# First attention of a decoder trunk: query weights loaded by whole depth, one unit for each group of heads, with the groups' scores placed between them

## The chip, the core and the metric

The kernel runs on one core of a Trainium2 chip. The core has a matrix engine (TensorE, PE in the profile, with its weight loads as PEld), VectorE (DVE), ScalarE (ACT), GpSimd (POOL) and an engine that issues most loads (SyncE, SP). The metric is the device time of one execution in microseconds; lower is better. Data lies in an on-chip memory of 128 partitions; TensorE writes its sums into eight banks, each of 128 partitions by 512 float32.

## The reference, cut to what matters

Two decoder layers and a final norm on x of shape (1, 256, 1024), all float32. Layer 0 is sliding-window attention with 16 heads of 64, 2 key and value heads, window 128, a learned sink logit per head and a relative bias, followed by a dense SwiGLU. Layer 1 is stick-breaking attention, followed by eight experts with top-2 routing. The change touches the first attention alone:

```
qkv = h @ w_qkv + b_qkv              # h = rms_norm(x): 256 x 1024, w_qkv: 1024 x 1280
q, k, v = split(qkv, [1024, 1152])   # 16 query heads, 2 key heads, 2 value heads of 64
s = einsum('bnqhgd,bnkhd->bnhgqk', q, kb) * 64 ** -0.5
s = where(valid, s + bias, -inf)     # kb: a block of 128 keys and the block before it
p = softmax(concat([s, sink]))[..., :-1]
o = einsum('bnhgqk,bnkhd->bnqhgd', p, vb)
x = x + o.reshape(...) @ w_o
```

## The kernel before, in words

**Weights come in units.** A unit is 1 MB of a weight matrix: 512 of its rows by 512 of its columns, or (what the code calls whole depth) all 1024 rows by 256 columns. SyncE loads a unit into one of seven `raw` buffers. ScalarE rounds it into `high` (`make_high`, L565), VectorE makes the remainder `low` = raw - high (`make_low`, L570), and TensorE multiplies with both: a product of float32 quality is three matmuls (high x high, high x low, low x high; L1542 stands for all matmuls that go through the helper). There are three `high` and three `low` buffers, so the rounding of unit n waits until TensorE has used unit n - 3, and the load of unit n waits until `low` of unit n - 7 is made. Units are numbered in the order of use: 0 and 1 hold the key and value columns (half as wide), 2 to 5 (`AT["q0"]` to `AT["q0"] + 3`) the query columns, 6 to 9 the output projection `wo0`, 10 and up the dense layer. `ENDS` says by which event a unit counts as used: a bank filled, or a count.

**Every engine has its own written order.** Each engine runs its program from top to bottom and waits on semaphores. `split_to(n)` in ScalarE's and VectorE's programs makes all units up to n that are not made yet, so where such a line stands decides what waits behind it. `plan()` assigns each result a bank and its turn in it; a writer waits until the bank's earlier contents are freed (`begin`), a reader until they are filled (`full`), and others until they are taken out (`taken`).

**The first attention.** The 16 heads are worked on in four groups g of four heads. For each group:

- TensorE fills `("q", g)` (256 query columns by 256 tokens).
- VectorE's `queries(g)` (L1191, L1196) scales it, adds the bias and writes `qT`.
- TensorE's `swa_scores(g)` fills four banks: `s1` (tokens 128 to 255 against 256 keys) and `s0` (tokens 0 to 127 against 128 keys).
- VectorE's `biased(g)` (L1208) adds bias and mask, which empties the banks; `shifts(g)` (L1218 to L1224) finds the rows' peaks.
- ScalarE takes the exponentials (L858).
- VectorE's `inverses(g)` (L1229 to L1231) and `probabilities` (L593) normalize; for group 1 GpSimd does the latter.
- TensorE's `swa_transpose(g)` (L1751) turns the probabilities into three banks, which ScalarE copies out (`probs_transposed`, L869).
- TensorE's `swa_values(g)` fills `("oT0", g)`, which ScalarE and VectorE split into the next product's input (`input_part_high` L827, `input_part_low` L1105).

The keys and values, each first turned upside down by a matmul (`keys_and_values_flipped`), come from VectorE's `kv_rows` (L1178); VectorE copies the keys into `kT_swa` (L1185) and the tokens' scale into `spread` (L1133).

Before the change, units 2 and 3 hold columns 0 to 511 of the queries (rows 0 to 511, then 512 to 1023), so groups 0 and 1 are both complete only near the end of unit 3, and the keys' flip stands between the two units. Then TensorE does `swa_scores(0)` and `swa_scores(1)`, units 4 and 5 (groups 2 and 3), `swa_scores(2)`, `swa_transpose(0)`, `swa_scores(3)`, `swa_transpose(1)`, `swa_values(0)`, `swa_values(1)` and unit 6, the first of `wo0`, which begins with the input that came from group 0 and needs group 1's from its third step of four. After unit 6 comes `swa_transpose(2)`, then unit 7, then `swa_transpose(3)` and the values of groups 2 and 3, then units 8 and 9.

**Loads around it.** SyncE's order is: x, units 0 and 1, the constants, units 2 and 3, then a wait for the bias rows (`rows_stored`: VectorE's table of 16 rows, written to memory by a GpSimd DMA), the load of `hankel` from them (16 x 128 pieces of 512 bytes on 128 partitions' side), units 4 and 5, `wo0`, and so on. GpSimd makes the bias mask from `hankel`.

Of the kernel before, what the change touches and what calls it, by code (L numbers as in the profile page):

```python
# [14 lines left out]
P = 128  # L15
# [57 lines left out]
def unit_ends():  # L73
# [4 lines left out]
    def add(name, *keys):  # L78
        at[name] = len(ends)
        ends.extend(keys)  # L80

    add("kv0", None, ("kv", 0))
    add("q0", None, ("q", 1), None, ("q", 3))
# [96 lines left out]
def plan():  # L180
# [6 lines left out]
    u.use("columns", 2)  # L187
    u.use(("R", 0), 1)
    u.use("k", 2)
    u.use(("q", 0), 4)  # L190
    u.use(("q", 1), 5)
    u.use("v", 6)

    def swa_scores(g, banks):
        for half in range(2):
            u.use(("s1", g, half), banks[half])
        for half in range(2):
            u.use(("s0", g, half), banks[2 + half])
# [4 lines left out]

    swa_scores(0, (0, 1, 2, 7))
    swa_scores(1, (3, 6, 4, 5))
    u.use(("q", 2), 0)
    u.use(("q", 3), 1)
    swa_scores(2, (2, 7, 3, 6))
    swa_transposes(0, (4, 5, 0))
    swa_scores(3, (2, 7, 3, 6))  # L210
    swa_transposes(1, (1, 4, 5))
    u.use(("oT0", 0), 0)
    u.use(("oT0", 1), 2)
    for tb, bank in enumerate((7, 3)):
        u.use(("wo0", 0, tb), bank)
    swa_transposes(2, (1, 5, 0))
    for tb, bank in enumerate((6, 4)):
        u.use(("wo0", 1, tb), bank)
    swa_transposes(3, (1, 5, 0))
    u.use(("oT0", 2), 2)  # L220
    u.use(("oT0", 3), 1)
# [98 lines left out]
def build(nc, a):  # L320

    ctx = ExitStack()
    with ctx:
# [280 lines left out]
        def _(sp):  # L604
# [39 lines left out]
            columns(AT["q0"], w, 0, HALF)  # L644
# [3 lines left out]
            columns(AT["q0"] + 2, w, HALF, 2 * HALF)  # L648
# [99 lines left out]
        def _(act):  # L748
# [95 lines left out]
            split_to(AT["kv0"] + 1 + SPLIT)  # L844
            b = full(act, "v")
            freed(nc.scalar.copy(v_swa[:, :, :].rearrange("p t s -> p (t s)"), b[:, 0:TB * KV * HD]), "v")
            split_to(AT["q0"] + SPLIT)
# [28 lines left out]
            probs_transposed(1)  # L876
            exponentials(2, range(GROUP // 2), True)
            input_part_high("oT0", 0)
            input_part_high("oT0", 1)
# [150 lines left out]
        def _(dve):  # L1030
# [205 lines left out]
            split_to(AT["kv0"] + 1 + SPLIT)  # L1236
            dve.wait_ge(minus_sinks_ready, 1)
            queries(0)
            queries(1)
            biased(0)  # L1240
            shifts(0)
            split_to(AT["q0"] + SPLIT)
# [3 lines left out]
            inverses(0)  # L1246
            queries(3)
            split_to(AT["q0"] + 1 + SPLIT)
            inverses(1)
            biased(2)  # L1250
            shifts(2)
# [288 lines left out]
        def _(pe):  # L1540
# [188 lines left out]
            by_features([("q", 0), ("q", 1)], AT["q0"], keys_and_values_flipped)  # L1729
# [37 lines left out]

            taken(pe, "k")
            swa_scores(0)
            swa_scores(1)  # L1770
            by_features([("q", 2), ("q", 3)], AT["q0"] + 2)
            swa_scores(2)
            swa_transpose(0)
            swa_scores(3)
            swa_transpose(1)
            taken(pe, "v")
            swa_values(0)
            swa_values(1)
# [300 lines left out]
```

## Time and profile before

| | |
|---|---|
| time, median of 3 runs | 1384.54 us (1384.53 to 1385.44) |
| profiled execution, its own time | 1387.25 us |
| span of that execution, first to last instruction | 1385.4 us |
| mean granted TensorE clock | 0.994 |
| TensorE busy | 1365.2 us (99%) |
| VectorE busy | 1126.9 us (81%) |
| ScalarE busy | 921.1 us (66%) |
| `low` L570, 397 instructions | 898.2 us, 2274 ns each |
| read from memory | 421.57 MB |

The page has six parts: busy time by engine; the span in 40 slices; the DMA queues; the chain of work that ended last, followed back from the end; the costliest groups of instructions, each with the idle time of its engine before it and what ended it; and the DMA issues. The first attention lies between about 17 and 94 us of the span. In the slices a digit is a busy share in tenths, for PEclk the granted share of TensorE's full clock of 2.4 GHz. A busy TensorE is not one at its best rate: at half the clock it counts as busy too.

### The profile page before, as it was taken

The page shows a single profiled execution, that of the slowest core. Times are in us where ns is not written, and L with a number is a line of the kernel's source. Part 1 is how long each engine was busy: PE and PEld are TensorE (multiplying, and loading weights), DVE is VectorE, ACT ScalarE, POOL GpSimd, SP SyncE. Part 2 cuts the span into 40 slices and gives each one's busy share as a digit, 9 for nine tenths or more (in the row PEclk, how much of TensorE's full clock was granted, in tenths as well). Part 3 has the DMA queues.
Part 4 walks back from the last instruction along what each step waited for, and adds up shares of the span by engine and source line. Part 5 has one row for each costly group of instructions (what it writes and reads, how often), then busy time and mean ns, then how long its engine had stood idle before and what let it go on. Part 6 is the DMA issues. An engine that isn't in the chain of part 4 may idle for free.

```text
span 1385.4 us, 18580 instructions
## 1 busy us (share of the span) xinstructions
PE 1365.2 (99%) x6770; PEld 1138.3 (82%) x6770; DVE 1126.9 (81%) x893; ACT 921.1 (66%) x766; POOL 41.9 (3%) x39
## 2 busy tenths in 40 slices
PE   8899999999999999999999999999999999999997
PEld 7788888898778888888888888888888888888885
DVE  5867666576458888888888888888898888889886
ACT  5664433544546777777777777777777777777775
POOL 2000000000000000000100000000000000000000
PEclk9999999999999999999999999999999999999999
DMA  9455654755148999999999999999999999999993
GB/s 309 164 173 192 205 176 148 232 183 186 44 149 327 386 377 349 394 385 360 371 393 387 347 394 371 375 372 390 374 363 395 375 354 383 395 373 366 391 371 123
DMA packets 197321, 429.52 MB, mean 310 GB/s; under 512 B 7046, under 2 KB 36976, under 8 KB 197280
## 3 DMA queue, kind: packets, MB, share of 16 engines
q1 hardware_dynamic: 193776, 417.63, 82.9%
q0 software_dynamic: 2944, 10.16, 2.6%
q10 hardware_dynamic: 560, 1.16, 0.3%
q8 instruction: 28, 0.46, 0.1%
q14 instruction: 13, 0.11, 0.0%
HBM read 421.57 MB, written 7.36 MB: 310 GB/s over the span
## 4 chain that ended last, share of the span: by engine, by line
PE 92%; DVE 5%; issue 1%; ACT 1%; DMA 1%; DVEq 0%; SPq 0%
PE bank L1542 89%; DVE low L570 2%; PE bank L1987 2%; DMA raw<-in_swa_w_qkv 1%; PE bank L1956 0%; DVE work L1463 0%; PE bank L1585 0%; PE bank L1751 0%; DVE work L1208 0%; DVE peak L1218 0%; DVE h L1070 0%; DVE h L1208 0%; DVE qT L1191 0%; DVE h L593 0%; PE bank L1916 0%
## 5 line engine op out<-in xcount | busy, mean ns | idle before, releaser
L570 DVE TENSOR_TENSOR low<-raw,high 128x2048 fp32r<-128x2048 f32 (+1 forms) x397 | 898.2, 2274 | 168.7 <-ACT high L565 166.6
L565 ACT CAST high<-raw 128x2048 fp32r<-128x2048 f32 (+1 forms) x397 | 754.7, 1902 | 287.2 <-PE bank L1542 276.3
L1542 PE MATMUL bank<-high,inT 128*128 128x512 f32 (+1 forms) x2032 | 647.1, 391 | 6.6 <-DVE low L570 2.6
L1542 PEld LDWEIGHTS bank<-high,inT 128*128 128x128 f32 x2032 | 381.7, 188 | 87.9 <-DVE low L570 5.4
L1542 PE MATMUL bank<-low,inT 128*128 128x512 f32 (+1 forms) x1016 | 394.7, 388 | 0.0
L1542 PEld LDWEIGHTS bank<-low,inT 128*128 128x128 f32 x1016 | 191.7, 189 | 37.5
L1542 PE MATMUL bank<-high,hid_high 128*128 128x512 f32 x528 | 207.2, 393 | 0.0
L1542 PE MATMUL bank<-high,hid_low 128*128 128x512 f32 x528 | 205.7, 390 | 0.0
L1542 PE MATMUL bank<-low,hid_high 128*128 128x512 f32 x528 | 205.5, 389 | 0.0
L1542 PE MATMUL bank<-inT,high 128*128 128x512 f32 (+1 forms) x704 | 190.7, 346 | 0.3 <-DVE inT L1114 0.3
L1542 PE MATMUL bank<-inT,low 128*128 128x256 f32 x544 | 144.4, 280 | 0.0
L1542 PEld LDWEIGHTS bank<-inT,high 128*128 128x128 f32 x704 | 119.1, 189 | 14.2 <-issue 0.7
L1542 PEld LDWEIGHTS bank<-high,hid_low 128*128 128x128 f32 x528 | 99.1, 188 | 21.0
L1542 PEld LDWEIGHTS bank<-low,hid_high 128*128 128x128 f32 x528 | 99.2, 188 | 20.2
L1542 PEld LDWEIGHTS bank<-high,hid_high 128*128 128x128 f32 x528 | 99.2, 188 | 19.9
L1542 PEld LDWEIGHTS bank<-inT,low 128*128 128x128 f32 x544 | 103.0, 189 | 4.1
L999 ACT ACTIVATE work<-bank 128x512 f32<-128x512 f32 x56 | 33.6, 599 | 45.9 <-PE bank L1542 45.9
L1442 DVE TENSOR_TENSOR hid_low<-bank,hid_high 128x512 fp32r<-128x512 f32 x56 | 38.3, 683 | 0.0
L1463 DVE TENSOR_TENSOR work<-work,bank 128x512 f32<-128x512 f32 x56 | 38.1, 681 | 0.0
L982 ACT CAST hid_high<-bank 128x512 fp32r<-128x512 f32 x56 | 32.6, 583 | 2.8 <-PE bank L1987 2.8
L1987 PEld LDWEIGHTS bank<-consts,work 128*128 128x128 f32 x224 | 27.8, 139 | 7.2
L1987 PE MATMUL bank<-consts,work 128*128 128x128 f32 x224 | 33.5, 271 | 0.0
(194 smaller groups left out, 536.8 us busy)
## 6 DMA issues: line engine op xcount, KB each, us to landing
raw<-in_moe_w_gate SPq DMA_DIRECT2D x112, 1024.0 KB, 7.2
raw<-in_moe_w_up SPq DMA_DIRECT2D x112, 1024.0 KB, 7.5
raw<-in_moe_w_down SPq DMA_DIRECT2D x112, 1024.0 KB, 7.3
raw<-in_sb_w_qkv SPq DMA_DIRECT2D x12, 1024.0 KB, 5.1
raw<-in_ffn_w_down SPq DMA_DIRECT2D x11, 1024.0 KB, 4.9
raw<-in_ffn_w_gate SPq DMA_DIRECT2D x10, 1024.0 KB, 5.4
raw<-in_ffn_w_up SPq DMA_DIRECT2D x10, 1024.0 KB, 5.3
raw<-in_swa_w_qkv SPq DMA_DIRECT2D x4, 1024.0 KB, 11.1
```

What stands on the lines that cost most here:

```text
L565: nc.scalar.copy(high[n % SPLIT][:, :, 0:c], raw[r][:, :, 0:c]).then_inc(high_done, 1)
L570: nc.vector.tensor_tensor(low[n % SPLIT][:, :, 0:c], raw[n % RAW][:, :, 0:c], high[n % SPLIT][:, :, 0:c].bitcast(F32), ALU.subtract).then_ ...
L982: nc.scalar.copy(hid_high[:, half_of(b)], p).then_inc(input_high_ready, 1)
L999: freed(nc.scalar.activation(e_silu[b % 2], p[0:CAP, :], ACT.Silu), ("g", b))
L1442: freed(V.tensor_tensor(hid_low[:, half_of(b)], bank[:, USES[("hidT", b)][0], :], hid_high[:, half_of(b)].bitcast(F32), ALU.subtract), ("h ...
L1463: freed(V.tensor_tensor(e_prod[b % 2], e_silu[b % 2], p[0:CAP, :], ALU.mult), ("u", b))
L1542: return nc.tensor.matmul(out, lhsT, rhs, start=start, stop=stop, **kw)
L1987: ins = nc.tensor.transpose(out[:, s * CAP:(s + 1) * CAP], e_prod[b % 2][:, s * P:(s + 1) * P], ident[0:CAP, 0:CAP])
```

## The change

It does the following.

- The four query units become whole-depth units, each of 256 columns, one for each group: `deep_columns` in place of `columns`. Each run of memory that a load reads is 1 KB in place of 2 KB; the bytes are the same. A unit counts as used when its group's bank is filled.
- TensorE has `queries_of(g, middle)`: the two column halves of group g, 24 matmuls each, with `middle` between them. The middle of group 0 is the flip of keys and values; that of groups 1, 2 and 3 is the scores of the group before.
- `swa_scores(3)` still follows `swa_transpose(0)`; `swa_values(0)` now stands ahead of `swa_transpose(1)`.
- Banks are dealt out anew. The scores of groups 2 and 3 both use 2, 7, 3, 0.
- VectorE: `queries(0)` now precedes the remainder of unit 4, `queries(1)` follows `shifts(0)`, `biased(2)`, `inverses(1)`, `shifts(2)` precede `queries(3)`, and the remainder of unit 6 follows `queries(3)`.
- ScalarE: the copy of the values precedes the rounding of unit 4, and the first half of group 2's exponentials and group 0's input part precede the copies of group 1's transposes.

```
@@ unit_ends
-    add("q0", None, ("q", 1), None, ("q", 3))
+    add("q0", *[("q", g) for g in range(H // GROUP)])
@@ plan
+    u.use(("q", 0), 4)
+    u.use("k", 2)
+    u.use("v", 6)
     u.use(("R", 0), 1)
-    u.use("k", 2)
-    u.use(("q", 0), 4)
-    u.use(("q", 1), 5)
-    u.use("v", 6)
...
+    u.use(("q", 1), 5)
     swa_scores(0, (0, 1, 2, 7))
-    swa_scores(1, (3, 6, 4, 5))
-    u.use(("q", 2), 0)
+    u.use(("q", 2), 3)
+    swa_scores(1, (4, 5, 6, 0))
     u.use(("q", 3), 1)
-    swa_scores(2, (2, 7, 3, 6))
-    swa_transposes(0, (4, 5, 0))
-    swa_scores(3, (2, 7, 3, 6))
+    swa_scores(2, (2, 7, 3, 0))
+    swa_transposes(0, (4, 5, 6))
+    swa_scores(3, (2, 7, 3, 0))
+    u.use(("oT0", 0), 6)
     swa_transposes(1, (1, 4, 5))
-    u.use(("oT0", 0), 0)
-    u.use(("oT0", 1), 2)
+    u.use(("oT0", 1), 1)
...
@@ SyncE
-            columns(AT["q0"], w, 0, HALF)
+            deep_columns(AT["q0"], w, 0)
             sp.wait_ge(rows_stored, 16)
...
-            columns(AT["q0"] + 2, w, HALF, 2 * HALF)
+            deep_columns(AT["q0"] + 2, w, HALF)
@@ ScalarE
-            split_to(AT["kv0"] + 1 + SPLIT)
             b = full(act, "v")
             freed(nc.scalar.copy(v_swa[:, :, :].rearrange("p t s -> p (t s)"), b[:, 0:TB * KV * HD]), "v")
+            split_to(AT["kv0"] + 1 + SPLIT)
             split_to(AT["q0"] + SPLIT)
...
             probs_transposed(0)
-            probs_transposed(1)
             exponentials(2, range(GROUP // 2), True)
             input_part_high("oT0", 0)
+            probs_transposed(1)
             input_part_high("oT0", 1)
@@ VectorE
-            split_to(AT["kv0"] + 1 + SPLIT)
             dve.wait_ge(minus_sinks_ready, 1)
             queries(0)
-            queries(1)
+            split_to(AT["q0"] + 2)
             biased(0)
             shifts(0)
-            split_to(AT["q0"] + SPLIT)
+            queries(1)
+            split_to(AT["q0"] + 3)
             biased(1)
             shifts(1)
             queries(2)
             inverses(0)
+            biased(2)
+            inverses(1)
+            shifts(2)
             queries(3)
             split_to(AT["q0"] + 1 + SPLIT)
-            inverses(1)
-            biased(2)
-            shifts(2)
             biased(3)
@@ TensorE
-            by_features([("q", 0), ("q", 1)], AT["q0"], keys_and_values_flipped)
+            def queries_of(g, middle):
+
+                w = unit(AT["q0"] + g)
+                wh, wl = by_tiles(w[0]), by_tiles(w[1])
+                b = begin(pe, ("q", g))
+                for s in range(2):
+                    cols = slice(s * P, (s + 1) * P)
+                    for t in range(DT):
+                        ins = product(b[:, s * SEQ:(s + 1) * SEQ], (wh[:, t, cols], wl[:, t, cols]), inputs(t, every),
+                                      s == 0 and t == 0, t == DT - 1, skip_group_check=True)
+                    if s == 0:
+                        middle()
+                filled(ins, ("q", g))
...
+            queries_of(0, keys_and_values_flipped)
             taken(pe, "k")
-            swa_scores(0)
-            swa_scores(1)
-            by_features([("q", 2), ("q", 3)], AT["q0"] + 2)
-            swa_scores(2)
+            queries_of(1, lambda: swa_scores(0))
+            queries_of(2, lambda: swa_scores(1))
+            queries_of(3, lambda: swa_scores(2))
             swa_transpose(0)
             swa_scores(3)
-            swa_transpose(1)
             taken(pe, "v")
             swa_values(0)
+            swa_transpose(1)
             swa_values(1)
             from_heads(0)
```

## Rows read from the trace of the kernel before

**Rows 1.** The page: engines' shares of the chain of work that ended last.

```profile
PE 92%; DVE 5%; issue 1%; ACT 1%; DMA 1%; DVEq 0%; SPq 0%
```

**Rows 2.** TensorE's waits to 130 us: line, releaser, total us, times, longest.

```profile
PE bank L1542 <- DVE work L1208: 2.8, 1, 2.8
```

**Rows 3.** Chain that ended last, 15 to 80 us: start, length, what.

```profile
17.42 15.90 PE bank L1542 x130
...
53.81 2.93 PE bank L1542 x16
...
57.38 1.56 ACT work L869 x3
...
59.05 1.73 ACT work L858 x8
60.78 0.48 ACT inT L827
...
62.13 5.71 PE bank L1542 x24
...
69.14 5.73 PE bank L1542 x24
...
79.13 0.93 PE bank L1542 x3
```

**Rows 4.** Windows: length, busy of PE, PEld, DVE, ACT, POOL; clock; DMA share, GB/s.

```profile
53.35:56.76 3.41, 2.95 (x17) 2.51 (x18) 3.21 (x8) 0.00 (x0) 2.38 (x3) 0.50 0.98 303
...
406.00:408.00 2.00, 2.00 (x7) 1.48 (x8) 0.72 (x5) 2.00 (x2) 0.00 (x0) 0.50 0.97 381
```

**Rows 5.** Timeline of VectorE: start, length, line, out<-in, count, idle before it.

```profile
26.72 1.73 DVE L1185 COPY kT_swa<-bank 64x256 f32<-64x256 f32 x4 [3.06 <-PE bank L1542]
...
34.60 1.95 DVE L1208 TENSOR_TENSOR h<-bank,kv_area 128x512 f32<-128x512 f32 x4
36.68 1.22 DVE L1218 TENSOR_REDUCE peak<-h 128x4 f32<-128x1024 f32 x1
...
38.81 2.28 DVE L570 TENSOR_TENSOR low<-raw,high 128x2048 fp32r<-128x2048 f32 x1
41.01 1.94 DVE L1208 TENSOR_TENSOR work<-bank,kv_area 128x512 f32<-128x512 f32 x4
...
45.22 0.68 DVE L1191 TENSOR_TENSOR qT<-bank,gain_row 128x512 f32<-128x512 f32 x1
...
46.47 0.16 DVE L1229 TENSOR_TENSOR total<-row_sum,sink_exp 128x8 f32<-128x8 f32 x1
...
48.65 0.68 DVE L1191 TENSOR_TENSOR qT<-bank,gain_row 128x512 f32<-128x512 f32 x1
```

**Rows 6.** Timeline of TensorE, 74 to 80 us.

```profile
74.71 1.47 PE L1751 MATMUL bank<-consts,h 128*128 128x128 f32 x12
76.11 1.52 PE L1542 MATMUL bank<-work,v_swa 128*64 128x256 f32 x12
77.46 1.47 PE L1542 MATMUL bank<-h,v_swa 128*64 128x256 f32 x12
```

**Rows 7.** DMA view, 12 to 15 us: packets of 2 KB.

```profile
DMA packets 585, 1.17 MB, mean 388 GB/s; under 512 B 16, under 2 KB 16, under 8 KB 585
```

**Rows 8.** DMA view, packets of 1 KB: 254 to 257, then 264 to 266.8 us.

```profile
DMA packets 1042, 1.07 MB, mean 356 GB/s; under 512 B 15, under 2 KB 1041, under 8 KB 1041
...
DMA packets 931, 0.94 MB, mean 336 GB/s; under 512 B 11, under 2 KB 931, under 8 KB 931
```

**Rows 9.** DMA view, 15 to 16 us: first packets of GpSimd's queue since 12.

```profile
q0 software_dynamic: 46, 0.04, 11.2%
```

**Rows 10.** Timeline of SyncE: the load of hankel, issued after the bias rows' store.

```profile
16.94 0.37 SPq L646 DMA_DIRECT2D work<-bias_dram  x1
```

**Rows 11.** Timeline of ScalarE: the rounding of unit 4.

```profile
26.82 1.91 ACT L565 CAST high<-raw 128x2048 fp32r<-128x2048 f32 x1 [5.48 <-DMA raw<-in_swa_w_qkv]
```

**Rows 12.** Timeline of GpSimd: the last piece of the bias mask.

```profile
26.67 1.08 POOL L714 TENSOR_SCALAR_AFFINE_SELECT kv_area<-work 128x1024 f32<-128x1024 f32 x1
```

More of the change, by code:

```diff
@@ L202, in swa_transposes @@
             u.use(("pT", g, t), bank)
+    u.use(("q", 1), 5)
     swa_scores(0, (0, 1, 2, 7))
-    swa_scores(1, (3, 6, 4, 5))
-    u.use(("q", 2), 0)
+    u.use(("q", 2), 3)
+    swa_scores(1, (4, 5, 6, 0))
     u.use(("q", 3), 1)
-    swa_scores(2, (2, 7, 3, 6))
-    swa_transposes(0, (4, 5, 0))
-    swa_scores(3, (2, 7, 3, 6))
+    swa_scores(2, (2, 7, 3, 0))
+    swa_transposes(0, (4, 5, 6))
+    swa_scores(3, (2, 7, 3, 0))
+    u.use(("oT0", 0), 6)
     swa_transposes(1, (1, 4, 5))
-    u.use(("oT0", 0), 0)
-    u.use(("oT0", 1), 2)
+    u.use(("oT0", 1), 1)
     for tb, bank in enumerate((7, 3)):
         u.use(("wo0", 0, tb), bank)
-    swa_transposes(2, (1, 5, 0))
-    for tb, bank in enumerate((6, 4)):
+    swa_transposes(2, (4, 5, 2))
+    for tb, bank in enumerate((6, 1)):
         u.use(("wo0", 1, tb), bank)
-    swa_transposes(3, (1, 5, 0))
+    swa_transposes(3, (0, 4, 5))
     u.use(("oT0", 2), 2)
-    u.use(("oT0", 3), 1)
+    u.use(("oT0", 3), 4)
     def transposed(name, banks):
```

## The prediction

> **What bounds the kernel now.** I read the page first. TensorE carries 92% of the chain that ended last [rows 1]. So a change here pays only if it takes away a wait of TensorE or a stretch at low clock, or lets a waiting chain of other engines end sooner; the number of matmuls stays the same. Second, the waits of TensorE up to 130 us: one stands out, 2.8 us, released by VectorE's `biased` (L1208) [rows 2]. The chain shows which: TensorE stops after `swa_transpose(0)` and starts `swa_scores(3)` at 53.81, when `biased(2)` has emptied the banks [rows 3]. Those scores then take 2.93 us [rows 3], because the granted clock is 0.50 of full (1.2 GHz) from 53.35 to 56.76, after TensorE had stood still since 51.0 [rows 4]. Behind them ScalarE copies the transposes (57.38), does half of group 2's exponentials (59.05, 1.73 us) and only then group 0's input (60.78), so `wo0` starts at 62.13 [rows 3]. Third, the timeline of VectorE: from 34.60, when `biased(0)` starts, its pieces follow one another without a pause, but before that it idled 3.06 us until 26.72, waiting for the keys' flip [rows 5]. So the stretch from 34 to 54 us is VectorE's; TensorE only looks full because its units fit beside it. From 62.13 on, the units of `wo0` start at 62.13, 69.14 and 79.13 [rows 3], and behind that TensorE carries the chain and all loads are started by VectorE's progress. What is gained at 79.13 is therefore gained at the end, as long as nothing there depends on absolute time.
>
> **Durations that I use**, all start to start. A query unit is 48 matmuls; 130 matmuls took 15.90 us, 0.122 each [rows 3], so 5.87 us, half 2.93. Scores of a group: 2.93 us at half clock [rows 3], 1.5 at full. Transposes 1.40 (74.71 to 76.11), values 1.35 (76.11 to 77.46) [rows 6]. VectorE [rows 5]: `biased` 2.0 (34.60 to 36.68 with a gap of 0.1), `shifts` 2.13 (36.68 to 38.81), a remainder 2.20 (38.81 to 41.01), `queries` 1.25 (45.22 to 46.47), `inverses` 2.18 (46.47 to 48.65), 0.3 for group 1, whose products GpSimd does. ScalarE: a transpose's copy 0.5 (a third of 1.56), an input part 0.5, half the exponentials 1.75 [rows 3].
>
> **The loads.** The four query loads read 1 KB pieces instead of 2 KB. With the queue full, 2 KB packets move at 388 GB/s [rows 7], 1 KB packets at 356 and 336 [rows 8]; 1.05 MB takes 2.7 us against 2.95 to 3.1, so 0.25 to 0.4 more for each. I take 0.27, by the steadier window (356). Units 2 and 3 have slack: TensorE wants them at 20.2 and 27.2. But they are ahead of something on another queue. The store of the bias rows goes over GpSimd's queue, which moved nothing from 12 us until the SyncE loads had nearly drained at 15 to 16 [rows 9], and `hankel` is issued at 16.94, behind it [rows 10]. So 0.54 us of delay passes on to `hankel` and to unit 4, and its own load adds 0.27: ScalarE rounds unit 4 at 27.6 instead of 26.82, where it already waited 5.48 us for this load [rows 11]. Bounds: 0 if none of it passes on, 1.4 if packets of 1 KB go at 336 and the store waits a little longer. The mask that GpSimd makes from `hankel` is complete at 27.75 [rows 12]; half a microsecond to 1.4 later it is still ahead of `biased(0)`, which wants it at 31.7.
>
> **The new order, step by step.** TensorE: unit 2 from 20.2, flips in its middle (1.15), its end at 27.2 fills group 0. Middle 23.1, so keys are flipped 3 us sooner; VectorE copies them by 26.1 and makes `spread` by 26.5: its idle of 3.06 shrinks to about 0.7. VectorE: `queries(0)` 27.25 to 28.5; the remainder of unit 4 waits for ScalarE (27.6 + 1.85) and takes 29.5 to 31.7; `biased(0)` to 33.65 (before it began at 34.60), `shifts(0)` 35.8, `queries(1)` 37.1, remainder of 5 39.3, `biased(1)` and `shifts(1)` 43.4, `queries(2)` 44.6, `inverses(0)` 46.8, `biased(2)` 48.8, `inverses(1)` 49.1, `shifts(2)` 51.2, `queries(3)` 52.5. TensorE beside it: unit 3 with the scores of group 0 in its middle to 34.65, unit 4 with group 1's to 42.1, unit 5 with group 2's to 49.55, transposes to 51.0. The three middles are new waits inside a unit, and half a unit stands behind each: `queries(0)` is through 1.6 us before it is asked for, `queries(1)` 0.5, `queries(2)` 0.4. If one is late by up to 1.6 us it costs nothing, since VectorE takes group 3 only at 51.2 while TensorE offers it at 49.55. The freed banks cost nothing: `biased(2)` empties 2, 7, 3, 0 at 48.8, where it used to be the wait. Next late is `queries(3)`: scores of group 3 start at 52.6, after a stall of 1.7 us, instead of 53.81.
>
> At full clock those scores end at 54.1, `swa_values(0)` at 55.5, `swa_transpose(1)` at 56.9, ScalarE's last copy at 57.6 (group 0's input went before), `swa_values(1)` at 59.0. Half of group 2's exponentials now stand in ScalarE's empty time from 51.3 to 53.4, and group 0's input is ready when VectorE leaves `biased(3)` at 56.7. So `wo0` starts at 59.0, 3.1 us sooner. Not all of that stays. Unit 7 wants its remainder, and VectorE reaches it by way of group 1's input (59.6 to 60.2), `shifts(3)` 62.4, `inverses(2)` 64.55, remainder 66.75. TensorE is through unit 6 and its transposes at 66.1 and waits some 0.75. Unit 7 starts at 66.9 against 69.14, unit 8 at 66.9 + 5.72 + 1.40 + 2.70 = 76.7 against 79.13 [rows 3]. **Sum: 2.4 us**, of which about 1.4 is the half clock that no longer falls on scores, values and transposes. The remainder of unit 6, moved behind `queries(3)`, ends at 54.7, over 4 us before TensorE wants it; ScalarE's move of the values' copy costs 0.4 us inside its wait for unit 4. Against the profiled execution that is 1387.25 - 2.4 = 1384.85; that execution is 2.7 us over the median, so on the median, 1384.54 - 2.4 = 1382.1.
>
> The Trainium skill ("DMA: Bandwidth & Descriptors", section "Queues, rings and completion order") says that each DMA engine takes turns between the queues that have work, packet by packet. By that rule the bias rows' store would not wait for units 2 and 3, and 0.54 us of the delay would be gone. The trace speaks against it here [rows 9]. The same page's "Specifications" gives 512 bytes as the smallest piece at line rate; by that the 1 KB pieces would cost nothing, and the trace shows a tenth more [rows 7, 8].
>
> **The rivals.** (a) The loads delay nothing: unit 4 is rounded at 26.8, and `queries(0)` at 28.5 becomes the gate of its remainder, so the chain starts about 0.5 to 0.6 us sooner. Gain 2.9 to 3.0, 1381.6. For it: the delay is only worked out from other stretches. The two sections of the Trainium skill named above ("DMA: Bandwidth & Descriptors") together give this case. (b) The clock falls in the stall that remains. It is 1.7 us, against the 2.4 us of standing still (51.0 to 53.35) that went before the fall [rows 2, 4], and narrow transposes stand ahead of it in both. Half clock over scores, values and transposes moves unit 7 from 66.9 to 68.6: gain 0.7, 1383.8. Against it: a shorter stall. (c) More comes off than I count: TensorE at half clock around 406 to 408, in the router's stretch, where matmuls of 512 columns with no use but to keep it busy stand ahead of a product that is waited for [rows 4]. The half clock lasts there for several us; if the earlier start lets it begin later or end sooner by 3.4 us, the length of the stretch at 53.35, half of that, 1.7, is gained: 1384.54 - 2.4 - 1.7 = 1380.4. (d) The other side: the same place, the other sign. If the half clock holds for longer, it lies on the first gather and the first expert's matmuls, and each microsecond of it costs half a microsecond. A stretch as long as the one at 53.35, 3.4 us [rows 4], adds at most 1.7 and gives 1383.8, no loss. Slower than before begins where 4.8 us more of half clock are added, slower by over 0.2% at 10.3 us: three such stretches, 1384.54 - 2.4 + 5.1 = 1387.3. (e) The order does not do what it says: a middle waits by more than the 1.6 us of slack, because the first links (flip, `spread`, `queries`) take longer when interleaved. Each microsecond beyond costs one; at 4 it is no change.
>
> **How the numbers follow.** Forecast, 1382.1 (1381.2 to 1382.9 by the loads' bounds): 0.42. (a) 0.12. (b) 0.20. (c) 0.14. (d) 0.06, most of it over the line, since an event that upsets the clock there seldom costs one stretch alone. (e) 0.06, of which none loses over 0.2%. A measurement of this kernel tells about 0.2% (2.8 us) from no change, so faster means below 1381.8. A quarter of the forecast's own spread lies beyond that (0.1), two thirds of (a) (0.08) and all of (c) (0.14): 0.32 for faster. Slower has 0.05, from (d); the rest, 0.63, is within. The range takes the forecast, (a), (b) and the nearer part of (c): 1380.4 to 1384.9.
>
> **What the profile of the changed kernel would show.** The rounding of unit 4 at 27.6, `biased(0)` at 31.7, `queries(3)` ending near 52.5 with TensorE's wait before `swa_scores(3)` at 1.7 us and named after L1196 instead of L1208, full clock from 50 to 60, `wo0` starting near 59.0, a wait of 0.75 for the remainder of unit 7, and unit 8 near 76.7. It is wrong if unit 4 lands after 28.5, if the clock falls before 57, if a middle shows a wait of over 1.6 us, or if the 2.4 us at unit 8 are not there at 400 us.

## The result, and the profile of the changed kernel

| | runs | median us | lowest to highest | profiled execution, its span |
|---|---|---|---|---|
| before | 5 | 1384.55 | 1384.53 to 1385.44 | 1387.25, 1385.4 |
| changed | 5 | 1390.98 | 1389.10 to 1393.91 | 1389.1, 1387.0 |

The ratio is 1.0039, interval 1.0028 to 1.0051: the changed kernel is slower by 0.4%, 5.4 us by the ratio and 6.4 by the medians. The prediction was 1382.1, with 1380.4 to 1384.9 as its range, so it is wrong in sign, and the time lies outside the range. What follows looks for the place where some 6 us are lost.

The page of the changed kernel, engines' shares of the chain that ended last, the line that answers to [rows 1]:

```profile
PE 90%; DVE 6%; issue 2%; ACT 2%; DMA 0%; DVEq 0%; SPq 0%; ACTq 0%
```

TensorE has given up two points of the chain to other engines. Where, the waits of TensorE to 130 us in the changed kernel tell, which answer to [rows 2] (line, releaser, total us, times, longest):

```profile
PE bank L1542 <- DVE kT_swa L1185: 3.0, 1, 3.0
...
PE bank L1542 <- DVE qT L1196: 2.3, 1, 2.3
...
PE bank L1542 <- ACT work L869: 1.0, 1, 1.0
PE bank L1542 <- DVE low L570: 0.7, 1, 0.7
```

The wait of 2.8 us behind L1208 is gone, and the wait named after L1196, foretold with 1.7, is there with 2.3; the wait for the copies of the transposes (L869) and the one for the remainder of unit 7 are as small as foretold. But the largest wait is one that the prediction doesn't know: 3.0 us for the copy of the keys (L1185). The chain of the changed kernel, 15 to 90 us (start, length, what; answers to [rows 3]):

```profile
16.15 6.86 PE bank L1542 x56
...
23.30 1.92 ACT high L565
25.25 1.14 DVE low L570
...
27.54 0.41 DVE kT_swa L1185
...
29.32 5.70 PE bank L1542 x31
...
56.98 4.64 PE bank L1542 x28
...
73.45 5.74 PE bank L1542 x24
...
83.44 6.61 PE bank L1542 x28
```

In [rows 3] one piece of TensorE runs from 17.42 through all of this. Here the chain leaves TensorE at 23.0, at the flip in the middle of unit 2, goes over ScalarE's rounding of a unit (23.30), VectorE's remainder of it (25.25) and the copy of the keys (27.54), and only at 29.32 comes back to TensorE. ScalarE's timeline says which units these are (start, length, line, out<-in, count, idle before and its releaser):

```profile
23.03 0.37 ACT L845 COPY v_swa<-bank 128x256 f32<-128x256 f32 x1 [3.81 <-PE bank L1542]
23.30 3.73 ACT L565 CAST high<-raw 128x2048 fp32r<-128x2048 f32 x2
```

ScalarE stands idle for 3.81 us until TensorE has flipped the values, copies them, and then rounds **two** units in a row, 3 and 4 (3.73 us; one takes 1.91 in [rows 11]). In the kernel before, unit 3 was rounded long before the copy:

```profile
19.44 1.89 ACT L565 CAST high<-raw 128x2048 fp32r<-128x2048 f32 x1
...
28.63 0.36 ACT L846 COPY v_swa<-bank 128x256 f32<-128x256 f32 x1
```

VectorE and TensorE behind it, in the changed kernel:

```profile
25.25 2.37 DVE L570 TENSOR_TENSOR low<-raw,high 128x2048 fp32r<-128x2048 f32 x1 [4.28 <-ACT high L565]
27.54 1.72 DVE L1185 COPY kT_swa<-bank 64x256 f32<-64x256 f32 x4
...
29.32 0.54 PE L1542 MATMUL bank<-inT,high 128*128 128x256 f32 x2 [3.02 <-DVE kT_swa L1185]
...
56.98 2.93 PE L1542 MATMUL bank<-kT_swa,qT 64*128 64x256 f32 x16 [2.26 <-DVE qT L1196]
```

VectorE's program has the remainder of unit 3 (`split_to(AT["q0"] + 1)`) ahead of the keys' copy, and TensorE has `taken(pe, "k")` ahead of unit 3: it may not go on until the keys are copied. The windows of the changed kernel (columns as in [rows 4]):

```profile
29.64:33.06 3.42, 3.42 (x18) 3.42 (x17) 3.35 (x5) 2.86 (x2) 0.00 (x0) 0.50 1.05 386
56.95:60.36 3.41, 3.38 (x20) 2.61 (x22) 3.41 (x4) 0.71 (x4) 0.00 (x0) 0.50 0.04 10
...
406.00:408.00 2.00, 2.00 (x15) 1.52 (x14) 1.64 (x5) 1.69 (x4) 0.00 (x0) 1.00 0.03 8
```

The granted clock is 0.50 (1.2 GHz) behind both stalls (a stall is a wait in which TensorE stands still), and full around 407, where it was 0.50 in [rows 4]. So the clock fell once more than before in the first attention, and not in the router's stretch.

**A common zero.** Executions differ by up to 1.6 us in when the first attention begins at all (18.67 to 20.31 us in the profiles below). I therefore count from the start of TensorE's unit 2, the first query unit; nothing of the change lies ahead of it but the loads. In before and in the changed kernel that is (one row of each kernel's TensorE timeline):

```profile
20.31 0.40 PE L1542 MATMUL bank<-inT,high 128*128 128x256 f32 x2
```

```profile
19.06 0.40 PE L1542 MATMUL bank<-inT,high 128*128 128x256 f32 x2
```

Unit 8 stands at 79.13 - 20.31 = 58.82 before [rows 3] and at 83.44 - 19.06 = 64.38 after: 5.6 us later. That is the size of the measured loss. Within the two profiled executions only 1.6 of it are left in the span, and two rows of each kernel say why, the first transposes of the router's stretch and the first matmul on its slots. Before:

```profile
399.84 1.91 PE L1916 MATMUL bank<-consts,x 128*128 128x128 f32 x16
...
417.62 0.51 PE L1542 MATMUL bank<-token,work 128*128 128x3 f32 x4
```

After:

```profile
404.16 1.91 PE L1928 MATMUL bank<-consts,x 128*128 128x128 f32 x16
...
419.39 0.51 PE L1542 MATMUL bank<-token,work 128*128 128x3 f32 x4
```

The stretch takes 17.78 us before, with the clock at half for 6.8 us of it, and 15.23 after, at full clock. So 2.55 of the 5.56 come back there in this execution, and 1.25 more is the earlier start: 5.6 - 2.55 - 1.25 = 1.8, about the 1.6 seen. The stretch differs from execution to execution: the profiled one is the fastest of the five, and in the profiles below it takes 16.1 or 17.8 us with both orders, and 15.2 in three more of the new one (e1, e8, e10). That is 4 of 10 profiles of the new order and none of 4 of the old, too few to say whether the change has a part in it. If it has, it gains time there and doesn't explain the loss.

### The profile page after: what moved, and what is told of

It is laid out like the page before. It is cut to its first block, busy times and chain, and to the rows that moved or that the text cites. A ratio compares the mean times of both kernels' runs of the same rounds, so it can differ in the third digit from the quotient of the medians.

```text
span 1387.0 us, 18603 instructions
## 1 busy us (share of the span) xinstructions
PE 1364.7 (98%) x6770; PEld 1138.0 (82%) x6770; DVE 1127.7 (81%) x893; ACT 921.5 (66%) x766; POOL 43.3 (3%) x39
## 4 chain that ended last, share of the span: by engine, by line
PE 90%; DVE 6%; issue 2%; ACT 2%; DMA 0%; DVEq 0%; SPq 0%; ACTq 0%
PE bank L1542 87%; DVE low L570 2%; PE bank L1999 2%; ACT high L565 1%; PE bank L1968 0%; DMA raw<-in_swa_w_qkv 0%; DVE peak L1218 0%; DVE work L1463 0%; DVE work L1208 0%; DVE h L1070 0%; PE bank L1585 0%; DVE peak L1219 0%; DVE h L1208 0%; DVE qT L1196 0%; DVE qT L1191 0%
```

## The experiments

Theory: **ScalarE's move of the values' copy carries the whole loss**, since `split_to` makes all units up to its argument, 3 as well as 4, and both now wait for the flip. Rivals: the 1 KB loads come late; the new order of VectorE and the middles inside the units cost more than they give; the clock. All of e1, e4 to e8, e11 and e12 put ScalarE's line back, so that the rest can be seen. Each was measured beside before on the same chip; the median of before was 1385.78 us beside e1 to e4, 1385.77 beside e5 to e8 and 1384.9 beside e9 to e12. "Scores" is the start of `swa_scores(3)`, counted like units 7 and 8 from the start of unit 2, read from the timeline of TensorE in each profile; half clock says whether the granted clock was 0.50 for a while at or just behind those scores. Positions are of one profile each and good to 0.01 or so; medians and ratios are of all timed executions. The ratio compares a kernel with before; one whose interval holds 1 isn't told from no change, and two kernels with overlapping intervals aren't told from each other.

| kernel | median | ratio, interval | scores | unit 7 | unit 8 | half clock |
|---|---|---|---|---|---|---|
| before | | | 33.50 | 48.83 | 58.82 | yes |
| changed | 1390.98 | 1.0039, 1.0028 to 1.0051 | 37.92 | 54.39 | 64.38 | yes |
| e1_round_first | 1384.81 | 0.9997, 0.9988 to 1.0006 | 33.23 | 48.12 | 58.12 | no |
| e2_before_late_round | 1391.58 | 1.0046, 1.0032 to 1.0059 | 39.50 | 54.90 | 64.89 | yes |
| e3_before_1kb | 1385.99 | 1.0006, 0.9997 to 1.0015 | 33.60 | 49.08 | 59.08 | yes |
| e4_unit7_early | 1385.43 | 1.0001, 0.9992 to 1.0010 | 33.25 | 48.81 | 58.79 | yes |
| e5_inverse1_early | 1384.86 | 1.0001, 0.9992 to 1.0010 | 33.01 | 47.90 | 57.89 | no |
| e6_inverse1_late | 1386.38 | 1.0010, 1.0001 to 1.0019 | 32.28 | 49.43 | 59.45 | no |
| e7_busy_stall | 1383.90 | 0.9992, 0.9983 to 1.0001 | 33.18 | 48.06 | 58.07 | no |
| e8_all_three | 1382.87 | 0.9988, 0.9979 to 0.9997 | 32.91 | 46.89 | 56.88 | no |
| e9_before_busy | 1382.92 | 0.9985, 0.9976 to 0.9994 | 33.50 | 47.67 | 57.67 | no |
| e10_keys_first | 1389.12 | 1.0032, 1.0020 to 1.0043 | 35.27 | 51.68 | 61.68 | yes |
| e11_queries3_early | 1381.62 | 0.9976, 0.9967 to 0.9985 | 31.23 | 46.39 | 56.38 | no |
| e12_queries3_late | 1386.59 | 1.0015, 1.0007 to 1.0024 | 34.86 | 51.36 | 61.36 | yes |

### e1: the changed kernel with ScalarE's line where it was

```
+            split_to(AT["kv0"] + 1 + SPLIT)
             b = full(act, "v")
             freed(nc.scalar.copy(v_swa..., b[:, 0:TB * KV * HD]), "v")
-            split_to(AT["kv0"] + 1 + SPLIT)
```

> The changed kernel with one line of ScalarE's program put back: the rounding of units 3 and 4 again ahead of the copy of the values. Theory 1 (the move made unit 3 wait for the keys' and values' flip, and the keys' copy behind its remainder): TensorE's wait of 3.0 us for the keys' copy near 29 us is gone, and with it the half clock behind it; scores of group 3 start near 52.6, unit 8 near 77, time 1382 to 1384. Theory 2 (the scores between the halves of the units, or the loads in 1 KB pieces, cost the time): the wait shows elsewhere and the time stays at 1388 to 1391.

Ratio 0.9997 against 1.0039: this one line is worth 0.42%, 5.8 us; unit 8 comes 6.26 us sooner. Timelines of e1, ScalarE, VectorE, TensorE:

```profile
19.51 1.89 ACT L565 CAST high<-raw 128x2048 fp32r<-128x2048 f32 x1
...
23.64 1.73 DVE L1185 COPY kT_swa<-bank 64x256 f32<-64x256 f32 x4
...
25.82 1.92 ACT L565 CAST high<-raw 128x2048 fp32r<-128x2048 f32 x1 [4.42 <-DMA raw<-in_swa_w_qkv]
...
52.30 1.58 PE L1542 MATMUL bank<-kT_swa,qT 64*128 64x256 f32 x16 [2.28 <-DVE qT L1196]
...
57.77 1.52 PE L1542 MATMUL bank<-work,v_swa 128*64 128x256 f32 x12 [0.98 <-ACT work L869]
...
67.19 0.50 PE L1542 MATMUL bank<-high,inT 128*128 128x512 f32 x1 [0.67 <-DVE low L570]
77.19 0.47 PE L1542 MATMUL bank<-high,inT 128*128 128x512 f32 x1 [0.21 <-DVE inT L1105]
```

Unit 3 is rounded at 19.51 again and unit 4, alone, at 25.82; the keys are copied at 23.64 instead of 27.54; TensorE doesn't wait ahead of unit 3. At the scores the difference to the changed kernel is 37.92 - 33.23 = 4.69: the wait of 3.02 and 1.7 for 3.42 us at half clock behind it. The other 1.6 is the half clock behind the second stall, which e1 doesn't have in this profile. So of the 6.26 us at unit 8 some 1.6 are the luck of this profile; the 5.8 us of the ratio come from eleven executions. The median, 1384.81, is a little above the 1382 to 1384 expected. The theory holds, and the rest of the change is worth nothing that can be measured: the interval reaches from 1.7 us of gain to 0.8 of loss, and the 2.4 us foretold lie outside it.

### e2: that one edit in the kernel before

```
-            split_to(AT["kv0"] + 1 + SPLIT)
             b = full(act, "v")
             freed(nc.scalar.copy(v_swa..., b[:, 0:TB * KV * HD]), "v")
+            split_to(AT["kv0"] + 1 + SPLIT)
```

> The kernel before with that one move alone: the copy of the values ahead of the rounding of units 3 and 4. Theory 1: unit 3 is rounded only after the flips at 27.1, its remainder ends near 31.5 where TensorE wants it at 27.2, so TensorE waits about 4.4 us and everything behind it is as much later: 1388.5 to 1391. Theory 2: no difference, 1384.5.

Alone it costs 0.46%, 6.4 us, as much as the whole change. ScalarE's timeline and TensorE's waits in e2:

```profile
26.12 5.50 ACT L565 CAST high<-raw 128x2048 fp32r<-128x2048 f32 x3
```

```profile
PE bank L1542 <- DVE low L570: 5.2, 2, 4.1
```

In before the flip stands behind unit 2, not in its middle. Behind the copy ScalarE now rounds three units without a pause (5.50 us): 3 and 4, which the moved line holds back, and 5. TensorE waits 4.1 us for unit 3's remainder, near the 4.4 expected.

### e3: the loads alone

```
-            columns(AT["q0"], w, 0, HALF)
+            deep_columns(AT["q0"], w, 0)
-            columns(AT["q0"] + 2, w, HALF, 2 * HALF)
+            deep_columns(AT["q0"] + 2, w, HALF)
```

> The kernel before with the four query units read by whole depth (1 KB pieces) and all else as it was; the product then takes weights in a wrong arrangement, so the queries are other numbers than the reference's, with the same work. By the prediction's step: unit 4 is rounded at 27.6 instead of 26.8, its remainder starts at 29.5 instead of 28.9, and time is 1384.5 to 1385.2. If the loads are what costs the time: unit 4 after 29 and 1387 or more.

TensorE's order isn't changed with the loads, so the queries are made of other columns of the weights; the work is the same. The time is that of before, within 0.15%. ScalarE's rounding of unit 4 and the DMA view of 12 to 15 us in e3 (the second line is GpSimd's queue: packets, MB, share):

```profile
26.08 1.91 ACT L565 CAST high<-raw 128x2048 fp32r<-128x2048 f32 x1 [4.38 <-DMA raw<-in_swa_w_qkv]
```

```profile
DMA packets 1035, 1.04 MB, mean 348 GB/s; under 512 B 16, under 2 KB 1035, under 8 KB 1035
...
q0 software_dynamic: 2, 0.00, 0.2%
```

The rate with a full queue is 348 GB/s against 388 [rows 7], as foretold, and again GpSimd's queue moves next to nothing while the loads run. Unit 4 is rounded 26.08 - 19.37 = 6.71 us after the start of unit 2, against 26.82 - 20.31 = 6.51 before: 0.2 later, where the prediction had 0.8. The loads don't carry the loss: the interval leaves them 2.1 us at most.

### e4 to e7: what is left of the new order, one term each, on top of e1

e4, the remainder of unit 7 ahead of group 1's input part (VectorE):

```
             input_part_low("oT0", 0)
+            split_to(AT["q0"] + 2 + SPLIT)
             input_part_low("oT0", 1)
...
-            split_to(AT["q0"] + 2 + SPLIT)
```

> As e1_round_first, with the remainder of unit 7 moved into VectorE's empty time between group 0's and group 1's input parts. If that remainder is what TensorE waits for before unit 7 (0.7 us in the changed kernel), the wait is gone and the time is 0.5 to 0.8 us below e1_round_first. If the row's normalization behind it is as late, the transposes of group 2 wait instead and nothing is gained.

The wait of 0.67 for unit 7's remainder is gone, but the time is that of before and not the 0.5 to 0.8 below e1 that was expected. In its profile the clock is at half from 52.4 for 3.4 us, behind a stall of the same 2.28 us that left it full in e1, though the two programs differ only behind this point. So this run doesn't tell what the move is worth.

e5, the inverses of group 1 ahead of `biased(2)`; e6, behind `queries(3)`:

```
+            inverses(1)
             biased(2)
-            inverses(1)
```

```
-            inverses(1)
             shifts(2)
             queries(3)
+            inverses(1)
```

> As e1_round_first, with VectorE's inverses of group 1 ahead of biased(2), so that GpSimd's products for group 1 run about 2 us sooner. In e1_round_first one instruction of 8 elements (L1224) took 0.97 us instead of 0.17 and ended when GpSimd's product ended. If VectorE's instructions with two inputs in on-chip memory wait for GpSimd's, L1224 is at 0.17 again and group 3's scores start 0.4 to 0.8 us sooner after unit 2 (33.2 us in e1_round_first); time 0.3 to 0.8 us lower. If the 0.97 has another cause, it stays.

> As e1_round_first, with the inverses of group 1 after queries(3), right ahead of the remainder of unit 6, whose two inputs are both in on-chip memory. If such an instruction waits for GpSimd's product of 2.9 us, that remainder or the next one of its kind lasts some 2.5 to 2.9 us longer, group 3's biased part is as late, and the time is 1 to 2.5 us above e1_round_first. If there is no such wait, the remainder stays at 2.3 us and the time is the same.

Both ask what `inverses(1)` does where it stands, since it starts GpSimd's product for group 1. VectorE and GpSimd in e1:

```profile
48.08 2.89 POOL L593 TENSOR_TENSOR work<-work,inverse 128x1024 f32<-128x1024 f32 x2 [20.26 <-DVE inverse L1231]
...
50.03 0.97 DVE L1224 TENSOR_TENSOR sink_gap<-shift,minus_sinks 128x8 f32<-128x8 f32 x1
```

In e5:

```profile
51.08 0.17 DVE L1224 TENSOR_TENSOR sink_gap<-shift,minus_sinks 128x8 f32<-128x8 f32 x1
```

In e6, the same two engines, and TensorE's wait:

```profile
51.66 2.24 DVE L570 TENSOR_TENSOR low<-raw,high 128x2048 fp32r<-128x2048 f32 x1
...
51.83 4.82 POOL L593 TENSOR_TENSOR work<-work,inverse 128x1024 f32<-128x1024 f32 x2 [23.87 <-DVE inverse L1231]
```

```profile
PE bank L1763 <- POOL work L593: 2.2, 1, 2.2
```

The small L1224 takes 0.97 us instead of 0.17 and ends at 51.00, just when GpSimd's product does (48.08 + 2.89 = 50.97). With the product earlier (e5) it takes 0.17 again, and the scores start 0.22 sooner; the rest goes to a wait of 0.36 for ScalarE's exponentials and to the product's new place. The time of e5 is that of e1, not 0.3 to 0.8 lower. With the product later (e6) it is the other way round, and not as expected: VectorE's remainder runs at its usual length until 53.90, and GpSimd's product, begun at 51.83, takes 4.82 instead of 2.89: it ends at 56.65, 2.89 after 53.76, which is about the remainder's end. Now `swa_transpose(1)` waits 2.2 us for it, and the scores' 0.95 us of gain turn into 1.3 of loss at unit 8. Ratio 1.0010 with an interval that begins at 1.0001.

e7, TensorE kept busy in the stall with matmuls of no use:

```
 swa_transpose(0)
+keep_clock(("s1", 3, 0), 2)
 swa_scores(3)
```

> As e1_round_first, with two matmuls of 512 columns that compute nothing wanted, between the transposes of group 0 and the scores of group 3, in TensorE's wait of 2.3 us for queries(3). They take 1.75 us of that wait. If it is this stall that lets the clock fall in most runs, no half clock is seen between 50 and 60 us, and the median is 0.7 to 1.5 us below e1_round_first. If the clock falls seldom there or for another reason, the two medians agree within 0.5 us.

No half clock between 50 and 60 us, the times of e1 in the timeline, ratio 0.9992: a shade better than e1, whose timed executions spread from 1382.85 to 1387.49, but the two intervals overlap and this run doesn't show a gain by itself.

### e8: the edits of e4, e5 and e7 together

> The three edits together on e1_round_first: group 1's inverses early, unit 7's remainder in VectorE's empty time, two matmuls in the stall. If the three prices add (0.5, 0.7 and 1.0 us), the median is 2 to 2.5 us below e1_round_first and 2 to 3 us below the kernel before. If they share one slack (the stall of the next engine takes over), it is at most 1 us below e1_round_first.

Unit 8 at 56.88, 1.24 before e1, ratio 0.9988, 1.3 us below e1's: less than the 2 to 2.5 us of three prices that add, and a little more than one slack would give. It is the first version of the new order that beats before, by an interval that ends at 0.9997.

### e9: is the new order needed for that?

The kernel before, with nothing but three matmuls of no use (the trace records each as two, so six) between `swa_transpose(0)` and `swa_scores(3)`:

```
             swa_transpose(0)
+            keep_clock(("pT", 1, 0), 3)
             swa_scores(3)
```

> The kernel before with three matmuls of 512 columns that compute nothing wanted in TensorE's wait of 2.8 us ahead of the scores of group 3. If the half clock behind that wait (3.4 us in the profile of before) comes of standing still, it does not fall there, unit 8 starts 1.5 to 1.7 us sooner after unit 2 than 58.8, and the median is 1 to 1.7 us below the kernel before. Then a good part of what e8_all_three gains needs none of the change. If it falls all the same, nothing moves.

TensorE's timeline and a window in e9:

```profile
49.41 2.74 PE L1542 MATMUL bank<-consts 128*128 128x512 f32 x6
52.40 1.58 PE L1542 MATMUL bank<-kT_swa,qT 64*128 64x256 f32 x16 [0.25 <-DVE work L1208]
```

```profile
51.00:53.00 2.00, 1.75 (x9) 0.82 (x9) 1.92 (x5) 0.00 (x0) 1.83 (x1) 1.00 0.48 125
```

The granted clock is 1.00 from 51.0 on. The scores start when they did (33.50), but take 1.58 us instead of 2.93 [rows 3], and unit 8 comes 1.15 sooner. Ratio 0.9985: this is as good as e8. It prices the half clock that the prediction meant to save at 1.15 us at unit 8; the ratio gives 2.1 us, with an interval from 0.8 to 3.3. And it gives the fair comparison for the new order: with the clock at full in all three, before reaches unit 8 at 57.67, e1 at 58.12 and e7 at 58.07. **In these profiles the new order in itself is 0.40 to 0.45 us worse**, not 1.0 better as the prediction's sum had it; the medians are too wide to show so little.

### e10: the copy of the keys ahead of the late remainder

The changed kernel as it is, but VectorE's `split_to(AT["q0"] + 1)` moved behind the keys' copy and `spread_scales(0)`.

> The changed kernel as it is on ScalarE, with VectorE's copies of the keys and of the scale ahead of the remainder of unit 3. The late rounding (ending at 25.2) then costs only unit 3's own remainder: TensorE waits for that until 27.5 instead of for the keys until 29.3. If the prediction's missed chain is rounding of 3, remainder of 3, keys' copies, TensorE's wait is 3.0 - 1.75 = 1.3 us, and the time is 1.7 to 3.5 us below the changed kernel (the latter if the clock no longer falls there). If only the rounding counts, nothing changes.

TensorE and VectorE in e10:

```profile
25.76 2.68 DVE L570 TENSOR_TENSOR low<-raw,high 128x2048 fp32r<-128x2048 f32 x1 [0.54 <-ACT high L565]
...
28.54 0.47 PE L1542 MATMUL bank<-inT,high 128*128 128x256 f32 x2 [1.80 <-issue]
```

The wait ahead of unit 3 shrinks from 3.02 to 1.80; the profile names no releaser, but the remainder of unit 3 ends at 28.44, 0.1 ahead. So in the changed kernel the keys' copy is the gate that the profile names, and the remainder, which the late rounding holds back, would be one too. The wait was expected at 1.3; the remainder takes 2.68 us here instead of 2.29, and it starts while a piece of GpSimd's mask still runs (25.21 to 26.29). Unit 8 comes 2.7 us before the changed kernel's: 1.2 by the shorter wait, the rest, 1.5, is about what the half clock behind that wait cost, which e10 doesn't have. The ratio, 1.0032, is still a loss, and only 1.0 us below the changed kernel's with overlapping intervals: VectorE's order is at most a part of the loss, and undoing ScalarE's line removes all of it (e1).

### e11 and e12: where `queries(3)` belongs

e11 is e8 without the matmuls of no use, and with `queries(3)` ahead of `shifts(2)`. e12 is e1 with `queries(3)` and the remainder of unit 6 ahead of `inverses(1)`, `biased(2)` and `shifts(2)`.

```
 # e11, from inverses(0) on          # e12, from inverses(0) on
 inverses(1)                         queries(3)
 biased(2)                           split_to(AT["q0"] + 1 + SPLIT)
 queries(3)                          inverses(1)
 shifts(2)                           biased(2)
 split_to(AT["q0"] + 1 + SPLIT)      shifts(2)
```

> As e8_all_three without its two extra matmuls, with queries(3) ahead of shifts(2). TensorE offers group 3 about when VectorE leaves biased(2), so the stall before group 3's scores goes from 2.0 us to under 0.5 and they start 30.8 to 31.2 after unit 2 instead of 32.9. Group 2's exponentials are 1.25 us later in exchange, and VectorE is then busy without a pause up to unit 7's start. If VectorE's sum bounds the stretch, unit 8 starts at 56.0 to 56.5 instead of 56.9: 0.4 to 0.9 us gained. If the later exponentials hold up the values, unit 8 is at 57 or later.

> As e1_round_first, with VectorE's order for groups 2 and 3 as in the kernel before: queries(3), the remainder of unit 6, inverses(1), biased(2), shifts(2). VectorE then idles for group 3's queries (about 2.5 us) and TensorE's scores of group 3 wait for biased(2) as before: they start about 35.3 after unit 2 instead of 33.2, and the time is 1.5 to 3 us above e1_round_first. If the order of VectorE does not matter, it stays.

TensorE in e11, then TensorE's waits and VectorE's timeline in e12:

```profile
49.90 1.58 PE L1542 MATMUL bank<-kT_swa,qT 64*128 64x256 f32 x16 [0.26 <-DVE qT L1196]
...
56.13 1.52 PE L1542 MATMUL bank<-work,v_swa 128*64 128x256 f32 x12 [1.75 <-ACT work L869]
```

```profile
PE bank L1542 <- DVE work L1208: 3.9, 1, 3.9
```

```profile
48.89 0.69 DVE L1191 TENSOR_TENSOR qT<-bank,gain_row 128x512 f32<-128x512 f32 x1 [2.93 <-PE bank L1542]
```

In e11 the stall, 2.28 in e1, is down to 0.26, the clock stays at full there with no help, and the wait one step on, for ScalarE's copies of the transposes, grows from 0.98 to 1.75. Unit 8 is at 56.38, as expected. The gain over before is 3.3 us: **1381.62 us, ratio 0.9976, faster than both kernels**. It is the gain of all its moves together; how much of it is `queries(3)` alone was not measured. In e12 `queries(3)` is asked for before TensorE has filled its bank (VectorE idles 2.93), everything behind it is late, and the scores wait 3.9 us for `biased(2)`. Early is right only as far as the bank is there: behind `biased(2)`, not ahead of it.

## Why the prediction was wrong

**The step that failed** is the sentence "ScalarE's move of the values' copy costs 0.4 us inside its wait for unit 4". I took the length of the copy as its price, and one instruction as what stands behind it. The copy isn't ready to run: it waits for the flip in the middle of unit 2 (3.81 us of idle). And `split_to(AT["kv0"] + 1 + SPLIT)` isn't the rounding of unit 4 alone; it makes every unit up to it that isn't made, and unit 3 was one. Both facts were to be had: before the change ScalarE rounds two units between 17 and 29 us (19.44 and 26.82), and only the later, [rows 11], waits for a load. The price is 5.8 us by e1, 6.4 by e2. What came is what rival (e) names by its effect (the first links take longer), but with a wait of 3 us where rival (e) was given no case that loses over 0.2%. The chance of 0.05 for slower is the same mistake, since all of it was put on the router's clock.

**The loads.** Right in sign and in rate (348 GB/s, foretold 356), too large in effect: 0.2 us at unit 4 instead of 0.8, e3. The prediction passed the delay of two loads on in full; less arrived (0.2 in e3, 6.75 - 6.51 = 0.24 in e1). That unit 4 is rounded before 28.5 and that its load costs nothing in the end held.

**The middles.** Held. In e1 none of the three waits, and `biased(0)` starts at 30.43 - 19.07 = 11.36, foretold 31.7 - 20.3 = 11.4. Up to that point the schedule as worked out was right, with the one line undone.

**The stall ahead of the scores.** Foretold 32.3 for the scores, measured 33.23 in e1; stall 1.7, measured 2.28. Of the 0.9 us, 0.8 is L1224 at 0.97 beside GpSimd's product. The prediction priced `inverses(1)` at 0.3 "for group 1, whose products GpSimd does": right for its own length, wrong for what it starts. From the scores to `wo0` 6.92 us were measured instead of 6.4 (52.30 to 59.22): 0.28 is the wait for ScalarE's copies (0.98 instead of 0.7), the rest transposes and values at 1.53 and 1.45 instead of 1.4. The wait for unit 7's remainder was foretold with 0.75 and is 0.67. Another 0.2 comes between units 7 and 8. Together 58.12 instead of 76.7 - 20.3 = 56.4.

**The half clock.** Foretold at 1.4 us saved, it is worth 1.15 in before (e9). Rival (b), that it falls in the remaining stall, is real: behind stalls of 2.26 to 2.28 us it fell in the changed kernel, e4 and e10, and did not fall in e1. It fell behind the stalls of 2.8 us and more (before, e2, e3, e12). It did not fall behind 2.04, 1.31 and 0.26 (e5, e6, e11), nor behind a stall of 2.20 ahead of `swa_transpose(1)` in e6, and not where TensorE had matmuls in the stall (e7, e8, e9). In e3 and e12 it fell only about 1 us after the scores had begun (full until 54.0 and 55.05, scores at 52.97 and 54.05), in the others with them or up to 0.5 us before. So the length of the stall alone doesn't say when it falls, and with stalls of 2.3 us one execution decides nothing.

**The router's stretch.** Rival (c) names a thing that exists: from the first transposes to the slots it takes 15.2 us at full clock, 16.1 with 3.4 us at half (e9, 397.28 to 413.40) and 17.8 with 6.8. It changes with the execution, and whether with this change too stays open: 15.2 us was seen in 4 of 10 profiles of the new order and in none of 4 of the old. The changed kernel had this best case in its profile and is slower all the same. Rival (d), its opposite, was not needed.

**The decomposition.** "What is gained at 79.13 is gained at the end" held in the other direction: 5.6 and 6.1 us lost at unit 8 are 5.4 and 6.4 by the ratios (changed kernel, e2). Small differences do less well: e10 is 2.9 us late at unit 8 and 4.4 by its ratio, e9 1.15 early and 2.1 by its ratio, and e4 to e8 lie up to a microsecond from what unit 8 says.

## What to carry to other kernels

Price a moved instruction by when its own input is ready, not by its length, and expand every helper that stands behind it ("make all up to n") into the instructions that it issues at that point: what queues behind a wait on an engine that runs its program in order inherits the whole wait. Before rearranging an order to shorten a stall, look whether the stall's clock can be had by filling it (e9: one line, 0.15%), and then move the piece that is waited for to the first place where its input exists, not further (e11, which has two other moves as well: 0.24%; e12 shows too early). Compare profiles from an anchor inside the kernel, since executions differ more in their start and in the clock of one stretch than such a change is worth.

## What the runs showed of the hardware

Some instructions of VectorE and GpSimd stop one another: the one that starts second stands until the other is done, and the first keeps about its usual length. L1224, 128x8 elements, takes 0.97 us instead of 0.17 and ends with GpSimd's product (e1; 0.96 in the changed kernel, e4, e7 and e10 too); GpSimd's product takes 4.82 instead of 2.89 behind a remainder of VectorE that keeps its 2.24 (e6). In the changed kernel it shows a third time, GpSimd's piece of the mask beside the remainder at 25.25, which usually takes 1.08 [rows 12]:

```profile
25.44 3.14 POOL L714 TENSOR_SCALAR_AFFINE_SELECT kv_area<-work 128x1024 f32<-128x1024 f32 x1
```

25.44 + 3.14 = 28.58, 1.08 after 27.50, again about where the remainder ends. It was there before the change, too: the first piece of the mask beside the remainder that runs from 21.37 for 2.29 us. And it isn't only instructions with two tensors as input: in e1, the first L1196 of `queries(0)`, with one, takes 0.72 us instead of 0.35 beside GpSimd's last piece of the mask (26.74 to 27.82). Before, then e1:

```profile
22.90 1.71 POOL L711 TENSOR_SCALAR_AFFINE_SELECT kv_area<-work 128x1024 f32<-128x1024 f32 x1 [9.28 <-DMA work<-bias_dram]
```

```profile
27.26 0.98 DVE L1196 TENSOR_SCALAR qT<-qT,columns 128x256 f32<-128x256 f32 x2
```

Beside the same GpSimd instructions, VectorE's reductions (L1218, 1.22 us) and its instructions that read a bank (L1208, L1191) keep their usual lengths. The Trainium skill ("SBUF — State Buffer", section "Who interferes with whom") says that a VectorE instruction with two inputs in SBUF, the on-chip memory, contends with a GpSimd instruction that reads SBUF, since they share ports under an exclusive lock, and that issue order decides who blocks. The rows of L1224, the product and the mask agree with it; L1222, which has two such inputs as well and runs at 49.82 in e1, inside the product, is recorded with its usual 0.18, so the rule or the record doesn't hold for all.

After a stall of 2.3 us between narrow transposes and the scores, TensorE's clock stayed at 2.4 GHz in e1 and fell to 1.2 for 3.4 us in e4, whose program is the same up to there; this costs 1.15 to 1.7 us. What decides it in an execution stays open. The spread of the changed kernel, 1389.1 to 1393.9, is wider than that of before. The mean granted clock of each execution goes with its time: 0.995 in the shortest of the changed kernel and 0.991 in the longest, 0.999 in the two shortest of e1 and 0.995 in the longest. I take the spread for the sum of such events, but only the profiled executions show a clock row by row, so where they fall in the others is argued and not shown.
